# Splitting the output projection into rounded parts, and loading every expert behind it

## What is computed

```python
def hybrid_mixer(h, ...):
    z = h @ w_in
    ...
    y_conv = u @ w_conv_out
    ...
    y_delta = o.reshape(bsz, t_len, VAL_DIM).astype(h.dtype) @ w_gdn_out
    y = jax.nn.sigmoid(gate_c) * y_conv + jax.nn.sigmoid(gate_d) * y_delta
    return y @ w_out

def hierarchical_moe(h, ...):
    t = h.reshape(-1, d)
    group_p = jax.nn.softmax((t @ w_router_group) + b_router_group, axis=-1)
    exp_logits = ((t @ w_router_expert) + b_router_expert).reshape(n_tok, N_GROUPS, EXPERTS_PER_GROUP)
    ...
    for e in range(N_EXPERTS):
        hid = jax.nn.silu(t @ w_expert_gate[e]) * (t @ w_expert_up[e])
        out = out + combine[:, e:e + 1] * (hid @ w_expert_down[e])

x = x + hybrid_mixer(rms_norm(x, norm_mix_gain[l]), ...)
x = x + hierarchical_moe(rms_norm(x, norm_ffn_gain[l]), ...)
return rms_norm(x, final_norm_gain)
```

## Time and profile before

| what | us |
|---|---|
| median of 3 runs | 974.13 |
| lowest and highest of them | 972.68, 975.51 |
| the profiled execution, its own time | 975.37 |
| its span in the trace | 973.6 |
| TensorE busy in it | 852.3 (88%) |
| VectorE busy | 644.9 (66%) |
| ScalarE busy | 491.2 (50%) |
| GpSimd busy | 357.1 (37%) |

### The profile page before, as it was taken

The page is one execution under the profiler, slowest core; times in us unless marked ns, Lnnn a source line. Parts: engine busy times, 40 slices in busy tenths (PEclk is TensorE's granted clock), DMA queues, the critical chain, the costliest instruction groups (busy, mean ns, idle before and its releaser), DMA issues.

```text
span 973.6 us, 11909 instructions
## 1 busy us (share of the span) xinstructions
PE 852.3 (88%) x4386; PEld 669.7 (69%) x4386; DVE 644.9 (66%) x778; ACT 491.2 (50%) x641; POOL 357.1 (37%) x241
## 2 busy tenths in 40 slices
PE   4999999578868979999999999399999999999950
PEld 3888877478758878885878456267777777777730
DVE  5499424979968964741116212758889888888836
ACT  7555430333424313244532113168888888888832
POOL 6254541575245602212564000223534435343110
PEclk9999999798979969999999998599999999999985
DMA  8563222000000021041080703749999998999406
GB/s 290 194 217 87 87 87 87 1 1 1 1 0 1 1 87 66 21 173 65 23 308 0 279 25 122 278 170 361 353 371 379 364 370 347 351 368 343 169 11 258
DMA packets 49818, 163.53 MB, mean 168 GB/s; under 512 B 11192, under 2 KB 15304, under 8 KB 41198
## 3 DMA queue, kind: packets, MB, share of 16 engines
q1 hardware_dynamic: 42398, 152.41, 41.6%
q0 software_dynamic: 7376, 10.52, 3.2%
HBM read 154.51 MB, written 25.17 MB: 185 GB/s over the span
## 4 chain that ended last, share of the span: by engine, by line
PE 54%; DVE 10%; DMA 2%; ACT 2%; POOL 1%; issue 1%; POOLq 0%; DVEq 0%; SPq 0%; ACTq 0%
PE bank L388 13%; PE bank L390 13%; PE bank L389 13%; PE bank L686 6%; DVE arena L1533 4%; PE bank L731 3%; DVE arena L1584 1%; DMA h_lo<-low_h 1%; DVE arena L1855 1%; PE bank L589 1%; DVE gu_lo L1681 1%; PE bank L627 1%; PE bank L609 1%; PE bank L526 1%; PE bank L753 1%
## 5 line engine op out<-in xcount | busy, mean ns | idle before, releaser
L1681 DVE TENSOR_TENSOR gu_lo<-wgu,gu_hi 128x2048 fp32r<-128x2048 f32 x64 | 146.4, 2289 | 21.8 <-ACT gu_hi L1325 21.5
L986 POOL TENSOR_TENSOR w_lo<-arena,w_hi 128x1024 fp32r<-128x1024 f32 x36 | 89.4, 2490 | 166.0 <-ACT w_hi L1113 166.0
L1325 ACT ACTIVATE gu_hi<-wgu 128x2048 fp32r<-128x2048 f32 x64 | 122.1, 1909 | 19.0 <-DMA h2T_keep<-arena 10.1
L1533 DVE SCALAR_TENSOR_TENSOR arena<-arena 128x512 f32<-128x512 f32 x120 | 123.0, 1089 | 0.1
L999 POOL TENSOR_TENSOR arena<-arena 128x512 f32<-128x512 f32 x56 | 85.3, 1551 | 100.4 <-PE bank L526 41.3
L1069 POOL DMA_INDIRECT arena<-h_rows,row_idx x32 | 81.1, 2534 | 105.4 <-DVE row_idx L1752 88.6
L388 PE MATMUL bank<-h_hi,w_hi 128*128 128x512 f32 x288 | 116.3, 404 | 1.6 <-DMA h_lo<-low_h 1.6
L389 PE MATMUL bank<-h_lo,w_hi 128*128 128x512 f32 x288 | 114.1, 396 | 0.0
L390 PE MATMUL bank<-h_hi,w_lo 128*128 128x512 f32 x288 | 113.9, 396 | 0.0
L1075 POOL DMA_INDIRECT y_rows<-arena,row_idx x32 | 40.2, 1257 | 182.0 <-ACT arena L1364 182.0
L388 PE MATMUL bank<-gu_hi,heT_hi 128*96 128x512 f32 x256 | 103.4, 404 | 2.4 <-DVE heT_lo L1776 1.9
(11 more groups left out here) (298 smaller groups left out, 1647.7 us busy)
## 6 DMA issues: line engine op xcount, KB each, us to landing
wgu<-in_w_expert_gate_dram SPq DMA_DIRECT2D x32, 1024.0 KB, 9.1
wgu<-in_w_expert_up_dram SPq DMA_DIRECT2D x32, 1024.0 KB, 17.7
wd<-in_w_expert_down_dram SPq DMA_DIRECT2D x32, 1024.0 KB, 13.4
arena<-in_w_in_dram SPq DMA_DIRECT2D x8, 2048.0 KB, 8.5
arena<-in_x_dram SPq DMA_DIRECT2D x8, 512.0 KB, 7.1
y_rows<-arena SPq DMA_DIRECT2D x8, 512.0 KB, 9.9
arena<-in_w_in_dram SPq DMA_DIRECT2D x4, 1024.0 KB, 8.2
arena<-in_w_out_dram SPq DMA_DIRECT2D x2, 2048.0 KB, 10.2
```

Of the source, the lines that this page charges most:

```text
L986: gp.tensor_tensor(as_raw(w_lo[pslot(s)], s), raw(s), as_raw(w_hi[pslot(s)], s).bitcast(F32), ALU.subtract)\
L1325: act.activation(gu_hi[j % 2][:, :, ks, :], wgu[j][:, :, ks, :], ACT.Copy)\
L1533: ins = STT(out=acc[:, i, :], in0=upad[:, i, t:t + T], scalar=par[:, o + t:o + t + 1], in1=acc[:, i, :], op0=ALU.mult, op1=ALU.add)
L1681: TT(gu_lo[j][:, :, ks, :], wgu[j][:, :, ks, :], gu_hi[j % 2][:, :, ks, :].bitcast(F32), ALU.subtract)\
```

## The change

- **Output projection in parts.** The weights of each half go to `wo_raw`; ACT rounds them in four pieces per half (`wo_part`), placed between the `b_hi` blocks of the yd stage. The rests are made by DVE for half 0 (`wo_rest` inside the loop over the yd blocks) and by POOL for half 1 (behind its last `b_lo`). The gated sum goes to `y_sum`, ACT rounds it (`y_part`), DVE makes the rest (`y_rest`). PE runs `split_product`, three matmul instructions for each block in place of two.
- **Order on PE.** `h2_tile(c-1)` stands between the two halves of tile c, and `logits_tile(c-1)` right behind tile c. ACT's order of square, root and `h2T_copy` is as before. The transposed rows lie in another region.
- **Loads.** All loads of experts stand behind the whole output projection: first the gate and up weights of expert 0, then the store of the last `h2` tile, the rest of expert 0, experts 1 and 2, the store of `h2T_keep`, and, once this has landed and the logits are read, expert 3.
- **Expert 0's rest** is made by POOL in place of DVE, ahead of the first gather.
- **The wait on `h2T_keep`** is gone from ACT.
- **The load of `wab`** counts on `ld_small`, for which every waiter now wants five loads instead of four.

The diff, cut to its core:

```diff
             for c in range(NT):
+                cs = slice(c * P, (c + 1) * P)
                 for hf in range(NH2):
-                    n = cidx[f"wo{hf}"]
-                    if c == 0:
-                        wait(pe, *arrived[n])
                     b = begin(("wo", c, hf), ("x1_ready", c * NH2 + hf + 1))
                     for m in range(KT):
+                        if c == 0:
+                            wait(pe, f"wo_lo{hf}", m // 2 + 1)
                         if hf == 0 and c == 0:
-                            wait(pe, "y_ready", m + 1)
-                        ins = pe.matmul(b[:], yT[:, m, c * P:(c + 1) * P], at(place[n], KT, HALF)[:, m, :], start=(m == 0),
-                                        stop=(m == KT - 1))
+                            wait(pe, "y_lo", m + 1)
+                        ins = split_product(b[:], (y_hi[:, m, cs], y_lo[:, m, cs]), (wo_hi[hf][:, m, :], wo_lo[hf][:, m, :]),
+                                            m == 0, m == KT - 1)
                     end(ins, ("wo", c, hf), "wo_mm")
+                    if c > 0 and hf == 0:
+                        h2_tile(c - 1)
                 if c > 0:
-                    h2_tile(c - 1)
-                if c > 1:
-                    logits_tile(c - 2)
+                    logits_tile(c - 1)
             h2_tile(NT - 1)
-            logits_tile(NT - 2)
             logits_tile(NT - 1)
...
+        def wo_rest(eng, i, hf, done):
+            eng.wait_ge(S["wo_hi"], hf * KT // 2 + i + 1)
+            ks = slice(2 * i, 2 * i + 2)
+            eng.tensor_tensor(wo_lo[hf][:, ks, :], wo_raw[hf][:, ks, :], wo_hi[hf][:, ks, :].bitcast(F32), ALU.subtract)\
+                .then_inc(S[done], 1)
...
-            sp.dma_start(wab, win[:, :, C_AB:C_AB + 2 * H]).then_inc(S["ld_ab"], 16)
+            sp.dma_start(wab, win[:, :, C_AB:C_AB + 2 * H]).then_inc(S["ld_small"], 16)
...
-            wait(sp, "y_ready", KT)
-            for j in range(2):
-                expert_gu(0, j)
-                expert_dn(0, j)
-            for c in range(NT):
+            def h2_store(c):
                 wait(sp, "h2_ready", c + 1)
                 sp.dma_start(h2_rows[c * P:(c + 1) * P, :], h2[:, c, :]).then_inc(S["st_h2"], 16)
+            for c in range(NT - 1):
+                h2_store(c)
             wait(sp, "wo_mm", 2 * NT)
-            for j in range(2, UN):
+            expert_gu(0, 0)
+            h2_store(NT - 1)
+            expert_dn(0, 0)
+            for j in range(1, UN - 1):
                 expert_gu(0, j)
                 expert_dn(0, j)
             wait(sp, "h2T_ready", 2 * NT)
             sp.dma_start(h2T_keep, h2T.rearrange("p k n -> p (k n)")).then_inc(S["st_h2T"], 16)
+            wait(sp, "routed", 1)
+            wait(sp, "st_h2T", 16)
+            expert_gu(0, UN - 1)
+            expert_dn(0, UN - 1)
...
+            for i in range(KT // 2):
+                wo_rest(gp, i, 1, "wo_lo1")
...
+            for half in range(2):
+                gp.wait_ge(S["w_ghi"], half + 1)
+                ks = slice(half * KH, (half + 1) * KH)
+                gp.tensor_tensor(gu_lo[0][:, :, ks, :], wgu[0][:, :, ks, :], gu_hi[0][:, :, ks, :].bitcast(F32), ALU.subtract)\
+                    .then_inc(S["w_glo"], 1)
             gp.wait_ge(S["idx_ready"], 1)
...
-            act.wait_ge(S["ld_small"], 64)
+            act.wait_ge(S["ld_small"], 80)
...
+            def wo_part(i, hf):
+                wait(act, *arrived[cidx[f"wo{hf}"]])
+                if hf == 0:
+                    act.wait_ge(S["b_lo"], KT)
+                else:
+                    act.wait_ge(S["gate_mm"], 2 * KT)
+                ks = slice(2 * i, 2 * i + 2)
+                act.activation(wo_hi[hf][:, ks, :], wo_raw[hf][:, ks, :], ACT.Copy).then_inc(S["wo_hi"], 1)
+            def y_part(m):
+                act.wait_ge(S["y_ready"], m + 1)
+                act.activation(y_hi[:, m, :], y_sum[m], ACT.Copy).then_inc(S["y_hi"], 1)
             for i in range(2, 2 * KT):
                 branch_hi(i)
+                if 10 <= i < 14:
+                    wo_part(i - 10, 0)
+                if i >= 14:
+                    wo_part(2 * (i - 14), 1)
+                    wo_part(2 * (i - 14) + 1, 1)
+                if i >= 12:
+                    y_part(i - 12)
+            for m in range(4, KT):
+                y_part(m)
...
-            act.wait_ge(S["st_h2T"], 16)
             gu_hi_half(1, 0, 1, 0)
...
+            def y_rest(m):
+                v.wait_ge(S["y_hi"], m + 1)
+                TT(y_lo[:, m, :], y_sum[m], y_hi[:, m, :].bitcast(F32), ALU.subtract).then_inc(S["y_lo"], 1)
             for m_ in range(KT):
                 src = ready(v, ("yd", m_))
-                tell(TT(sig[1][:, m_, :], sig[1][:, m_, :], src[:], ALU.mult), "yd_ready")
-                v.wait_ge(S["yc_ready"], m_ + 1)
-                v.wait_ge(S["yd_ready"], m_ + 1)
-                TT(yT[:, m_, :], yT[:, m_, :], sig[1][:, m_, :], ALU.add).then_inc(S["y_ready"], 1)
+                tell(TT(sig[1][:, m_, :], sig[1][:, m_, :], src[:], ALU.mult), "yc_ready")
+                v.wait_ge(S["yc_ready"], KT + m_ + 1)
+                TT(y_sum[m_], yT[:, m_, :], sig[1][:, m_, :], ALU.add).then_inc(S["y_ready"], 1)
+                if m_ < KT // 2:
+                    wo_rest(v, m_, 0, "wo_lo0")
+                if m_ > 0:
+                    y_rest(m_ - 1)
+            y_rest(KT - 1)
...
-            gu_lo_half(0, 0, 0, 0)
-            gu_lo_half(0, 0, 0, 1)
```

More of the change, by code:

```diff
@@ L157, in hybrid_layer @@
         hidT_lo = parts("hidT_lo", R_E0 + JE * CAP, JE, CAP)
+        wo_at = [R_RING + WSLOT, R_U]
+        wo_raw = [parts(f"wo_raw{i}", o, KT, HALF, dt=F32) for i, o in enumerate(wo_at)]
+        wo_lo = [parts(f"wo_lo{i}", o, KT, HALF) for i, o in enumerate(wo_at)]
+        wo_hi = [parts(f"wo_hi{i}", o, KT, HALF) for i, o in enumerate((R_QK, R_SIG + KT * T))]
+        y_sum = [parts(f"y_sum{m}", R_SIG + m * T, T, dt=F32) for m in range(KT)]
+        y_lo = parts("y_lo", R_SIG, KT, T)
+        y_hi = parts("y_hi", R_QKT, KT, T)
         arena = ctx.enter_context(nc.sbuf_tensor("arena", [P, ARENA], F32))
@@ L240, in hybrid_layer @@
         hs = [at(o, D) for o in (R_UP + JE * D, R_UP + JE * D + D, R_S2, R_MASK)]
-        h2T = at(R_SIG + KT * T, KT, T)
+        h2T = at(R_RING, KT, T)
         h2 = at(R_UP, NT, D)
@@ L647, in _ @@
             for m in range(KT):
-                b = begin(("yd", m), ("yd_ready", m + 1))
+                b = begin(("yd", m), ("yc_ready", KT + m + 1))
                 wait(pe, "b_lo", KT + m + 1)
@@ L844, in load @@
                     return
-                sp.dma_start(at(place[n], src.shape[1], src.shape[2]), src).then_inc(S[arrived[n][0]], 16)
+                dst = wo_raw[int(chunks[n][0][-1])] if chunks[n][0][:2] == "wo" else at(place[n], src.shape[1], src.shape[2])
+                sp.dma_start(dst, src).then_inc(S[arrived[n][0]], 16)
             load(0)
@@ L1017, in _ @@
                     if grp == 0 and lv == 2:
-                        gp.wait_ge(S["ld_small"], 64)
+                        gp.wait_ge(S["ld_small"], 80)
                         for c in range(NT):
@@ L1113, in hi_part @@
                 act.activation(as_raw(w_hi[pslot(s)], s), raw(s), ACT.Copy).then_inc(S["w_hi"], 1)
-            act.wait_ge(S["ld_ab"], 16)
+            act.wait_ge(S["ld_small"], 80)
             act.activation(ab_hi, wab, ACT.Copy).then_inc(S["h_hi"], 1)
@@ L1258, in _ @@
                 act.wait_ge(S["oss"], c + 1)
-                act.activation(ors[:, c, :], oss[:, c, :], ACT.Sqrt, scale=1.0 / DK, bias=epsb).then_inc(S["ors"], 1)
+                act.activation(ors[:, c, :], oss[:, c, :], ACT.Sqrt, scale=1.0 / DK, bias=epsb).then_inc(S["osq"], 1)
                 if c > 0:
@@ L1430, in _ @@
                 TS(xs[:, c, :], xs[:, c, :], sm["r1"][:, c:c + 1], None, ALU.mult).then_inc(S["xs_ready"], 1)
-            v.wait_ge(S["ld_small"], 64)
+            v.wait_ge(S["ld_small"], 80)
             for k in range(KT):
@@ L1590, in output @@
             def output(c):
-                v.wait_ge(S["ors"], c + 1)
+                v.wait_ge(S["osq"], 2 * c + 2)
                 link(v.reciprocal(ors[:, c, :], ors[:, c, :]))
@@ L1640, in _ @@
                 dw(4 if c < NT - 1 else len(taps))
-                v.wait_ge(S["osq"], c + 1)
+                v.wait_ge(S["osq"], 2 * c + 1)
                 v.tensor_reduce(oss[:, c, :], heads(o_s), AX.X, ALU.add).then_inc(S["oss"], 1)
@@ L1805, in trip @@
                         gu_lo_half(e + 2, g2, j2, 0)
+            wait(v, "w_glo", 2)
             gu_lo_half(1, 0, 1, 0)
```

2 lines of the change are left out of this document (1 added, 1 removed).

## The result

| | kernel before | changed kernel |
|---|---|---|
| median, us | 974.31 (4 runs, 972.68 to 975.51) | 1003.98 (4 runs, 1001.97 to 1006.15) |
| the profiled execution, its own time | 975.37 | 1001.97 |
| its span | 973.6 | 1000.2 |
| ratio | | 1.0306, interval 1.0275 to 1.0338 |

The change makes the kernel 3.1% slower. The forecast was 1000, with a range of 983 to 1008 and 0.92 on slower.

The account below looks back on a forecast made before the run. PE was taken to bound the kernel (54% of the chain) until the output projection ends, then changing engines. The terms sum to +25.5 us: 975.4 + 25.5 = 1000.9, less 1.2 for the median, 1000; range 983 to 1008.

Parts of the forecast that it names:

- Matmuls: Output projection on PE: 192 new matmul instructions take 43.4 us where 128 fp32 ones took 55.0; gain 11.6.
- The start: Start of the kernel: ACT's first rounding waits for `wab`, so `h_hi` starts 1.9 us later; cost 1.9.
- The rests in the yd stage: yd stage: POOL's rests push back DVE's new instructions, so the last `y_lo` comes at 554.3; cost 10.7 us.
- The two new waits: Projection on PE: it stands 3.4 us behind tiles 1 and 2 for ACT's copies; cost 6.8.
- Clock: PE after the yd stage and after two later waits: a lower granted clock costs 2.2 us, three times: 6.6.
- Tail: Projection's end: transposes and logits moved ahead of it cost 2.6 us; the work behind it takes 10.5, net -1.6.
- Routing: Routing on DVE, 15.7 us: POOL's two rests of expert 0, 4.64 each, lie across it; cost 8.1 us.
- First gather: First expert's rows: the gather meets the end of the load queue of experts 0 to 2; cost 2.0 us.
- No exclusion: Rival, yd stage and routing: DVE and POOL share, or DVE always goes first; 980 us, chance 0.08.
- faster: Rival: DVE wins each meeting with POOL, `y_lo` 7 comes before 544 and PE's clock stays up; 970 us, chance 0.04.
- The loads decide: Rival: a longer load queue makes the gather take 9.4 us and expert 3 or 4 late; 1006 us, chance 0.10.

Follow-up runs that it names:

- ACT copies first: Changed kernel with ACT's copies of tile c-1's transposed rows put ahead of the square and root of tile c: 990.18 us, ratio 1.0158.
- PE's order as before the change: Changed kernel with the transposes and logits of a tile back at their old places in PE's program, ACT's order kept: 986.66 us, ratio 1.0136.
- the repaired one: Changed kernel with PE's old order, expert 0's rests on DVE, half 1 in yc, expert 3 and expert 1's rest later: 972.48 us; plus early down weights: 969.49.

## Why the prediction was right, step by step

The sum came to 1000.9 and the profiled execution took 1001.97. The mechanisms named are, but for the first gather's, those that the trace shows. That the sum came within 1.1 us is luck in part: by the rows of the table above its stretches missed by -3.6, +3.6, +1.9, -2.0 and +1.1.

- **Matmuls, -11.6.** Right. In the run with PE's old order a half tile at full clock takes 5.38 between two bank readings (594.38 to 599.76), before 6.80 (590.76 to 597.56): 8 times 1.42 is 11.4.
- **The start, +1.9.** Mis-sized, and unresolved. `h_hi` came at 15.1, but the first yd multiplication stood at 519.5 against 520.0 before. The step "nothing later in the chain is tied to a clock of its own" may still hold on average: 500 us of other waits vary by more than the term.
- **The rests in the yd stage, +10.7.** Right. DVE needed 33.9 us from the first yd multiplication to the last `y_lo`, 34.3 were predicted, and taking POOL's rests away gave back 7.3.
- **The two new waits, +6.8.** Right: 6.6. They come of PE's new order and ACT's old one together: putting either order back removes them (the runs "ACT copies first" and "PE's order as before the change").
- **Clock, 3 x 2.2.** Mechanism right, size wrong in its parts: 3.4 behind each inner wait, over the 3.0 that was given as the ceiling. Of these, the matmuls of the projection that run at half clock are 2.2 (the first ten take 4.4 us instead of 2.3), just what was forecast; what the sum lacked is the 16 logits matmuls, which stand behind the wait too and cost 1.2 more (2.9 us up to the next matmul instead of 1.7). Behind the yd stage only some 1.3: the second half tile took 6.2 and not 5.4, and the end of the first 2.4 and not 1.9 behind the last `y_lo`. In all 8.1 against 6.6. The row from which the term was taken was misread as well: there were no 8 us without matmuls ahead of 360. In the kernel before PE waited 2.85 us there and then ran small matmuls, under which the clock fell:

```profile
344.96 3.07 PE L555 MATMUL bank<-arena 128*128 128x128 f32 x16 [2.85 <-DVE arena L1584]
...
345.00:348.00 3.00, 3.00 (x17) 2.31 (x17) 3.00 (x6) 1.79 (x3) 0.00 (x0) 0.71 0.00 0
348.00:352.00 4.00, 4.00 (x42) 4.00 (x42) 4.00 (x7) 2.06 (x5) 0.00 (x0) 0.50 0.01 4
```

  So "the gaps are shorter than that of the row" was no reason to go below 3.0.
- **Tail, +2.6 and -1.6.** The first measured 2.9. The second was the step that failed most plainly: the tail became 0.3 longer. It had put the logits of tile 2 at full clock (1.7) and the last transposes at 1.3; behind the third wait the clock fell, and they took 2.7 (to the next matmul) and 1.9.
- **Routing, +8.1.** Measured 6.1, because POOL began 2.0 us before the routing reached it; where it met the routing in full it was 8.1. The prediction had cited the Trainium skill's page "SBUF — State Buffer", section "Who interferes with whom", for a lock over the whole instruction, and put its result near 9.3; the rows agree with the rule (DVE stands until a POOL instruction of 4.4 us is over); that it then gets just one turn is read from the rows. With ACT's copies first the amount is POOL's 8.95 less the 0.5 that had passed when DVE came to the first such instruction and less the 0.34 of its own two: 8.1.
- **First gather, +2.0.** Measured 3.1, by another cause than the one written down. Not the end of experts 0 to 2 but expert 3 stood ahead of it, which the prediction had coming at 43 us behind the projection and which was issued at 32 (646.87 less 614.63), 2.8 us ahead of the gather; held back, it left the gather 3.9 us. So the 2.0 was near by luck. The written cause became real as soon as the gather was issued 25 us behind the projection.
- **Rivals.** "No exclusion" (980) and "faster" (970) fell with the stretched rows. "The loads decide" was not this kernel's case; in the repaired one the loads behind the projection are 4 us of the gather (7.9 against 4.0).

## What to carry to other kernels

Before elementwise work goes to POOL because it is idle, look at what DVE does in that stretch: with both inputs in SBUF the two ran one after the other here, and only free time of both together counts. A wait of 3.3 us on PE in a stretch of matmuls had to be priced twice, once as itself and once as the half clock behind it (3.4), which also falls on whatever small matmuls stand there. When an operand split costs rounding work, do it in the stage where ACT and DVE both idle: the kernel that lost 3.1% is 0.6% faster than the one before with the work put there, PE's old order, expert 0's rests back on DVE and loads issued as their places come free.

## What the runs showed of the chip that was not expected

- DVE also holds POOL: issuing an indirect DMA takes POOL 0.97 us alone, 2.9 beside one rest of 2.29 on DVE and 5.07 beside two (with expert 0's rests on DVE). The same section of the Trainium skill's page "SBUF — State Buffer" tells of a probe in which a tensor-tensor instruction didn't stall a DMA of POOL's, and gives the reason as inferred; in the rows here the issue is stalled. This issue also reads `row_idx` out of SBUF. Whether that or the making of the transfer is what waits was not tested.
- The same 32 logits matmuls took 6.93 us or 3.68, at 1.2 or 2.4 GHz, after pauses of the same length (1.29 and 1.28, both ahead of the last transposes). What went before differed in form, fp32 against parts; which trait of it decides was not tested.
- Cutting POOL's instructions into quarters changed the longest DVE wait from 4.4 to 1.3 us and the sum of the waits hardly (21.6 to 21.1 us of routing).
- One row shows a TensorScalar with one input in SBUF held by POOL like the instructions with two (1.30 us, where POOL's rests are in eight pieces); a gate multiplication that reads a bank and a reduction weren't. The words "both inputs in SBUF" of the prediction are too narrow; that section of the Trainium skill has it so, with reductions free of contention and a scalar form that can take part, and the rows agree.
- Like code ran up to 3.4 us apart from its middle by 383 us; a term of 2 us in the first half of this kernel can't be read from a single trace.
